# Experts' gate and up weights in one transfer of 16 KB rows in place of two of 8 KB rows

## What is computed

```python
def swiglu(x, w_gu, w_down):
    g, u = jnp.split(x @ w_gu, 2, axis=-1)
    return (jax.nn.silu(g) * u) @ w_down

def expert_block(args):
    tok, e = args
    return swiglu(x_pad[tok], w_exp_gu[e], w_exp_down[e])
```

## Time and profile before

| | us |
|---|---|
| median of 3 runs | 1976.32 (1974.76 to 1976.75) |
| profiled execution | 1979.44 |
| its span | 1977.3 |
| TensorE busy | 1873.5 (95%) |
| VectorE busy | 957.8 (48%) |
| queue 1 | 55,728 packets, 303.59 MB |

### The profile page before, as it was taken

How to read it: one execution, slowest core, us unless ns; L and a number is a source line. 1 busy time by engine, 2 the same in 40 slices (tenths; PEclk the granted TensorE clock), 3 DMA queues, 4 the chain that set the end, 5 groups by cost and what they waited for, 6 DMA issues and landing times. The chain is left out here.

```text
span 1977.3 us, 28004 instructions
## 1 busy us (share of the span) xinstructions
PE 1873.5 (95%) x10606; PEld 1040.9 (53%) x10606; DVE 957.8 (48%) x2029; ACT 523.2 (26%) x1154; POOL 333.4 (17%) x297
## 2 busy tenths in 40 slices
PE   8999999999998999999999997999999999999997
PEld 3334448845443344444443343447756588888443
DVE  4987748733375232332332224713466554454643
ACT  2447831101311333333333332220255100000000
POOL 0655530000027110010010014400024000000000
PEclk9999999999999999999999999999999999999998
DMA  6129972203354999999999999704310122222311
GB/s 249 64 77 231 236 210 101 73 16 152 132 203 164 372 404 403 402 399 406 402 402 399 397 399 374 274 24 155 136 43 1 43 107 86 86 86 86 133 59 43
DMA packets 85536, 396.90 MB, mean 201 GB/s; under 512 B 13394, under 2 KB 13650, under 8 KB 60240
## 3 DMA queue, kind: packets, MB, share of 16 engines
q1 hardware_dynamic: 55728, 303.59, 39.8%
q10 hardware_dynamic: 16880, 58.52, 10.1%
q0 software_dynamic: 12848, 33.74, 4.6%
HBM read 374.66 MB, written 55.09 MB: 217 GB/s over the span
## 5 line engine op out<-in xcount | busy, mean ns | idle before, releaser
L2818 DVE COPY slab<-bank 32x512 f32<-32x512 f32 x124 | 80.9, 688 | 403.6 <-PE bank L1472 398.2
L1083 PE MATMUL bank<-ring,slab 128*128 128x512 f32 (+1 forms) x608 | 257.6, 584 | 6.5 <-DVE slab L2286 3.8
L1464 PE MATMUL bank<-slab 128*32 128x512 f32 x1536 | 230.7, 602 | 19.8 <-DMA ring<-w_exp_down 11.1
L1464 PE MATMUL bank<-ring,slab 128*32 128x512 f32 x1536 | 227.1, 595 | 15.4 <-DMA slab<-w_exp_down 7.0
L1472 PE MATMUL bank<-ring,slab 128*32 128x512 f32 x512 | 230.3, 603 | 0.0
L1472 PE MATMUL bank<-slab 128*32 128x512 f32 x480 | 212.6, 596 | 0.0
L1083 PEld LDWEIGHTS bank<-ring,slab 128*128 128x128 f32 x608 | 116.9, 194 | 141.0 <-issue 132.3
L3230 POOL TENSOR_TENSOR small<-small 128x1 f32<-128x1 f32 (+2 forms) x30 | 27.5, 921 | 818.4 <-DVE small L2283 818.4
L1464 PEld LDWEIGHTS bank<-slab 128*32 128x32 f32 x1536 | 73.0, 111 | 150.3 <-issue 143.1
L1083 PE MATMUL bank<-slab,ring 128*128 128x512 f32 (+1 forms) x368 | 148.2, 559 | 1.6 <-ACT slab L1826 0.9
L1464 PEld LDWEIGHTS bank<-ring,slab 128*32 128x32 f32 x1536 | 71.5, 110 | 145.1 <-issue 140.9
(11 more groups left out here) (363 smaller groups left out, 3050.6 us busy)
## 6 DMA issues: line engine op xcount, KB each, us to landing
ring<-stream SPq DMA_DIRECT2D x173, 512.0 KB, 4.4
slab<-w_exp_gu SPq DMA_DIRECT2D x64, 1024.0 KB, 14.4
ring<-w_exp_gu SPq DMA_DIRECT2D x64, 1024.0 KB, 14.3
ring<-w_exp_down SPq DMA_DIRECT2D x32, 1024.0 KB, 22.7
slab<-w_exp_down SPq DMA_DIRECT2D x32, 1024.0 KB, 23.4
y_rows<-zeros ACTq DMA_DIRECT2D x1, 24960.0 KB, 130.0
y_rows<-slab ACTq DMA_DIRECT2D x64, 384.0 KB, 8.3
gb<-rows ACTq DMA_DIRECT2D x5, 512.0 KB, 4.3
```

Of the source, the lines that this page charges most:

```text
L1083: mm = nc.tensor.matmul(dst, lhs[k], rhs[k], start=(k == 0), stop=(k == len(lhs) - 1))
L1464: mm = nc.tensor.matmul(g_bank[32 * g:32 * g + 32, :], x[:, k, 32 * g:32 * g + 32], w[:, 512 * k:512 * k + 512], start=(k == 0), stop=(k = ...
L2818: i = nc.vector.tensor_copy(ye[b % 2][32:64, 512 * half:512 * half + 512], bank[5 + half][96:128, :])
```

## The change

The two blocks of an expert's gate and up weights are laid side by side in the host's array, so that each partition's 16 KB lie in one piece: rows k = 0 to 7 of the eight 128-row steps, 2 KB each, one after another. One transfer of 128 rows of 16 KB replaces two of 128 rows of 8 KB. The place of every weight in the buffer stays as it was, so the products are unchanged. TensorE's wait counts 16 per expert in place of 32. The branch for experts with more than 96 tokens follows the new layout; it isn't run with these inputs.

```diff
             def gate_up_rows(e, j):
-                for h in range(2):
-                    sp.dma_start(gu_w[j][:, 2048 * h:2048 * h + 2048], a["w_exp_gu"][e][h]).then_inc(gu_landed[j], 16)
+                sp.dma_start(gu_w[j], a["w_exp_gu"][e]).then_inc(gu_landed[j], 16)
...
-                        sp.dma_start(gu_w[0].rearrange("p (h n) -> p h n", h=2), a["w_exp_gu"][bass.ds(e, 1)].rearrange("a h p n -> p (a h) n")).then_inc(ov["w"], 16)
+                        sp.dma_start(gu_w[0], a["w_exp_gu"][bass.ds(e, 1)].rearrange("a p n -> p (a n)")).then_inc(ov["w"], 16)
...
-                pe.wait_ge(gu_landed[b], 32 * u + 32)
+                pe.wait_ge(gu_landed[b], 16 * u + 16)
...
-        "w_exp_gu": w["w_exp_gu"][0].reshape(NE, 2, KD // 2, P, 2 * FF).transpose(0, 1, 3, 2, 4).reshape(NE, 2, P, KD * FF),
+        "w_exp_gu": w["w_exp_gu"][0].reshape(NE, KD, P, 2 * FF).transpose(0, 2, 1, 3).reshape(NE, P, 2 * KD * FF),
```

## The result

The changed kernel takes 1990.4 us (median of 7 runs, 1982.6 to 1992.3), the kernel before 1976.7 us beside it (7 runs, 1974.4 to 1979.9). The ratio is 1.0062 (95%: 1.0046 to 1.0078), so it is slower by some 12 us. The forecast was 1969.0, faster; its rival (c), the slower one, came true, and the time lies beyond the range. The profiled execution took 1990.4 us with a span of 1988.5. All times in this document are of executions in the chip's faster state; one of the evened kernel with 16 KB rows, at 2033.7 us and a granted clock of 0.94 in place of 0.98 to 0.99, fell in the slower one and is left out.

A forecast was written before the change was run, and what follows sets the result against it. TensorE was taken to set the pace first and late expert weights after, with about 14 us to win. Part 1 nothing, Part 2 4.8 and Part 3 2.6 us made 7.4 us off 1976.32: 1969, range 1963 to 1979.

The forecast's parts named there:

- rival (c): Weight loads: sixteen engines reading 16 KB pieces meet more often in memory; slower from 659 ns a row, 1983 at 674; chance 0.17.
- What bounds the kernel: Expert stretch: TensorE sets the pace, then late weights as the backlog grows 0.44 us per expert; about 14 us bound the gain.
- a copy of VectorE or ScalarE: Sign against the forecast: TensorE's pauses would move from the down weights to such a copy.
- Part 1: Expert weight loads: same bytes and order, wait at the same place, one SyncE issue fewer (about 0.45 us, hidden); costed at nothing.
- Part 2: Gate-up rows in the full stretch: 16 KB costs 644 ns (628 to 654); last down rows land 4.8 us earlier (0 to 12.5).
- 0.36 us per turn: Queue of expert weights while TensorE sets the pace: backlog growth slowed to this from 0.44 by saving 80 ns per expert.
- The packets of 46,512: Sign in the profile after: queue 1 has 9,216 packets fewer, leaving 46,512.
- a window in which nothing else ran: Load of `x_tm` at 289 to 293 us, the calm stretch: rows of 16 KB at 628 ns each.
- the 10 ns: Part 2's cost of a row beside its bytes in the full stretch: twice 169 less 327 ns.
- Part 3: Last experts, beside the combination's gathers: fewer weight rows let 8 gathered rows fewer ahead, 1.3 us per gate-up transfer, 2.6 us.
- 7.1 was forecast: Sign at the last experts: gate-up 63 lands 7.1 us behind down 60, in place of 8.4.
- the 10.1 that was allowed: Part 3's landing time for a store of `ye`, up from 8.3 us; under the 11.9 before rewriting, so cost nothing.

The follow-up runs named there:

- the evened kernel: Token slots dealt evenly over partitions, so each engine gets about 4 filled rows: kernel before (8 KB rows) 1970.9 us, 0.9954; changed kernel (16 KB) 1971.7 us, 0.9954.
- the 4 KB kernel: Kernel before with gate and up weights in four transfers of 128 rows of 4 KB per expert, in place of two of 8 KB: 1989.4 us, ratio 1.0041.
- the gathers replaced: Each token gather replaced by a plain transfer of 96 rows of 256 B: kernel before 1965.3 us, 0.9936; changed kernel 1961.1 us, 0.9912.

## Why the prediction was wrong

**What bounds the kernel** was read rightly: a backlog in queue 1 that eats its lead and then sets TensorE's pace. The loss stands in that wait. No pause moved to a copy of VectorE or ScalarE, and the granted clock was 1.00 in both windows.

**Part 1** held: neither the number of transfers, nor the issue, the grain of the wait or the array's order moved the time (1980.2 and 1981.7 against 1981.7). What it costed at nothing was 0.07 us per turn in favour of one transfer, as long as TensorE sets the pace.

**Part 2 is the step that failed**, by sign: 644 ns for a row of 16 KB in the full stretch, between ends of 628 and 654. It was 666 in 700:1000 and 689 in 1000:1180, so a long row costs 14 and 31 ns more than two short ones there, not 10 less. In growth of the backlog: 0.36 us per turn was forecast and 0.63 measured, where before had 0.44. The old rows in one transfer had 0.51, so some 0.12 us of the 0.63 go with the length, 15 ns for each of 8 rows, which fits the 14. That is an estimate: the growth differs by 0.1 us and more between kernels with the same rows (0.32 in the new array with rows of 8 KB, by landings of 14.3 us at 695.1 and 24.5 at 992.3). The packets of 46,512 came as forecast, so the change did what it says.

The mistake was to draw a line through rows of 4 and 8 KB, means over all engines, the 4 KB figure from stores and the 8 KB one from loads, and go on to 16 KB, and to hold it up with a window in which nothing else ran. Even the 10 ns weren't borne out as a cost: with 16 rows more per engine and expert the 4 KB kernel's down rows were no later than those of the kernels with 8 KB rows (22.8 us against 24.5 and 29.2). Both ends of the term were taken from those two sources, so the term had no end for a row dearer than two halves, though rival (c) had just that. The means also hid where the backlog is: in the kernel before five of the 16 engines had next to none, and the prediction knew that a gather gives an engine 4 to 6 rows, but used that only to ask how late the gather itself would be.

**Part 3** held for the order of the landings; its 2.6 us can't be found in the time. SyncE's timeline (start, length, instruction), last refills, and their landings in the order gate-up 62, down 60, gate-up 63, down 61:

```profile
1182.15 0.33 SPq L964 DMA_DIRECT2D slab<-w_exp_gu  x1
1183.05 0.33 SPq L967 DMA_DIRECT2D ring<-w_exp_down  x1
1192.34 0.33 SPq L964 DMA_DIRECT2D slab<-w_exp_gu  x1
1193.23 0.33 SPq L967 DMA_DIRECT2D ring<-w_exp_down  x1
```

```profile
slab<-w_exp_gu SPq DMA_DIRECT2D x1, 2048.0 KB, 28.6
...
ring<-w_exp_down SPq DMA_DIRECT2D x1, 1024.0 KB, 31.9
...
slab<-w_exp_gu SPq DMA_DIRECT2D x1, 2048.0 KB, 29.3
...
ring<-w_exp_down SPq DMA_DIRECT2D x1, 1024.0 KB, 32.5
```

Down 60 landed at 1183.05 + 31.9 = 1215.0, gate-up 63 at 1192.34 + 29.3 = 1221.6: 6.7 us apart, where 7.1 was forecast and 8.4 stood before. TensorE's pauses from 1195 us on, less the usual gap, are 5.4 - 1.1 = 4.3 us against 5.1. So the step was worth a microsecond or so and was swamped by Part 2. A store of `ye` took 10.4 us to land, a little over the 10.1 that was allowed, and still less than the 11.9 at hand.

**Rival (c)** names the right mechanism by its price: by its own rule a row of 666 to 689 ns, 12 to 35 over its 654, gives 8 x 60 x 12 to 35 ns = 5.8 to 16.8 us, less 2.6: 3 to 14, and 12 to 14 were measured. Its reason was half right. Contention is there, but most of it is not among the long rows alone: with evenly loaded engines queue 1 costs the same with long rows as with short ones (638 and 639 ns) or nearly (646 and 648 to 653). Its chance of 0.17 was too low, since the trace had a sign for it: a row in the full stretch at 654 ns for 16 KB against 628 in the calm one.

**What is not settled:** why long rows and unevenly loaded engines together are dearer than either, and why 0.11 us per turn stays with even ones. The queues take turns on each engine, and all 16 share the memory; which of the two hurts wasn't separated. That the loss falls on the late engines is read from their completions, 29.2 us against 32.7 where the early ones end alike; that they are late by the gathers' rows is argued from what evening them out does, since no run moved these rows to other engines while keeping them uneven. Why one transfer per expert makes TensorE's free turn 0.07 us shorter is open too.

## What to carry to other kernels

Price a changed transfer where it will run: with the other queues beside it, and on the DMA engine that lands last, not by a mean over 16 engines or a calm window; and put a bound on the bad side of a fit that leaves its data. Where an indirect gather skips empty slots, look at which engines its filled rows fall on: dealing them evenly gave 0.46% here, where no other row length gave anything. Longer rows are not better by themselves: rows of 8 KB had nothing to gain here from length, nor transfers of 1 MB from being merged.

## What the runs showed of the hardware that was not expected

- In the packet records of the full stretch the commonest times are 159, 309 and 611 ns for rows of 4, 8 and 16 KB, so 7 to 9 ns are fixed per row. Above that long rows have the thicker tail: from 700 to 1000 us 14% of the 8 KB rows of queue 1 take over 20 ns more in the kernel before, and 39% of the 16 KB rows in the changed kernel. The tail alone is no cost: with the gathers replaced it is 38%, at a mean of 709 ns, and nothing waits.
- The 16 parts of one transfer of 128 rows can end 20 us apart, when another queue loads the engines unevenly (997.8 us in the kernel before: 10.3 to 29.2 us); the semaphore shows only the last.
- With a tenth of the traffic taken away (stores cut) the DMA share stays at 101%, and queue 1 goes from 660 to 702 ns per 16 KB. A share at one doesn't say that the DMA binds: the waits for its transfers do. With the share at 1.02 the evened kernel had none.
- One core moved 409 GB/s in all in the evened kernel, weights, gathers and stores together, with no other core at work. The Trainium skill, DMA: Bandwidth & Descriptors, Specifications, has some 358 GB/s as the limit of HBM for one core; with 400 before and 409 evened it did not bind here.
